# Two weight rests of the output projection: from VectorE to GpSimd, in both layers of the first block

## The reference, cut to what matters

```python
p = jnp.einsum('btd,dc->btc', h, w_in[l])
pa, pb, pc, pd = _split(p, MIXER_COLS)
ya = _hgrn2_mixer(pa, ...); yb = _gla_mixer(pb, ...)
yc, v_first = _rwkv7_mixer(pc, ...); yd = _retnet_mixer(pd, ...)
mix = jnp.einsum('btc,cd->btd', jnp.concatenate([ya, yb, yc, yd], axis=-1), w_out[l])
h = _layer_norm(DN_ALPHA * h + mix, ln1_g[l], ln1_b[l])
```

## Time and profile before

| | |
|---|---|
| median of 3 runs | 3009.65 us |
| the profiled execution | 3002.6 us |
| its core's span | 3000.8 us |
| TensorE busy | 2778.2 us, 93% |
| VectorE busy | 1542.7 us, 51% |
| ScalarE busy | 1085.3 us, 36% |
| GpSimd busy | 208.7 us, 7% |
| mean granted TensorE clock | 0.95 of full |

### The profile page before, as it was taken

One profiled execution on the slowest core, in us unless ns is written; L12 is line 12 of the kernel. 1 busy time (PEld: TensorE's weight loads), 2 busy tenths in 40 slices (PEclk: granted clock), 3 DMA queues, 4 the chain that ended last, 5 costly groups with the idle time before them and its releaser, 6 DMA issues. The chain is left out here.

```text
span 3000.8 us, 38408 instructions
## 1 busy us (share of the span) xinstructions
PE 2778.2 (93%) x14780; PEld 2374.6 (79%) x14780; DVE 1542.7 (51%) x2136; ACT 1085.3 (36%) x1524; POOL 208.7 (7%) x205
## 2 busy tenths in 40 slices
PE   7999999999999999969999999949999896899999
PEld 5779877878877798858988888848878784788787
DVE  3526674232444366647777777763232516732333
ACT  2334223222233242225555555532122416431222
POOL 0011200000000112050000000210000002000000
PEclk9999999999999998879999999979999996899999
DMA  4310025142233000238888888953242210251521
GB/s 151 102 48 1 29 71 140 50 135 79 74 88 97 31 1 29 85 118 237 248 239 235 236 235 237 266 146 91 76 128 74 67 50 20 84 142 48 148 67 67
DMA packets 435565, 335.24 MB, mean 112 GB/s; under 512 B 23488, under 2 KB 375744, under 8 KB 435312
## 3 DMA queue, kind: packets, MB, share of 16 engines
q1 hardware_dynamic: 429360, 318.14, 36.8%
q0 software_dynamic: 3008, 10.09, 1.0%
q10 hardware_dynamic: 3072, 5.24, 0.5%
HBM read 323.43 MB, written 9.99 MB: 111 GB/s over the span
## 5 line engine op out<-in xcount | busy, mean ns | idle before, releaser
L2438 PE MATMUL psum<-x_split,gate_up_split 128*128 128x512 f32 x1056 | 416.5, 394 | 13.9 <-DVE h_tok L2548 5.3
L2439 PE MATMUL psum<-x_split,gate_up_split 128*128 128x512 f32 x1056 | 415.1, 393 | 0.0
L2440 PE MATMUL psum<-x_split,gate_up_split 128*128 128x512 f32 x1056 | 415.0, 393 | 0.0
L3510 PE MATMUL psum<-x_slots_split,gate_up_split 128*128 128x320 f32 x1424 | 378.2, 344 | 16.1 <-DVE gate_up_split L3731 12.4
L3511 PE MATMUL psum<-x_slots_split,gate_up_split 128*128 128x160 f32 x1424 | 314.4, 241 | 0.0
L2561 DVE TENSOR_TENSOR arena<-arena,psum 128x512 f32<-128x512 f32 x66 | 45.3, 687 | 517.0 <-ACT arena L2503 517.0
L3510 PEld LDWEIGHTS psum<-x_slots_split,gate_up_split 128*128 128x128 f32 x1424 | 260.7, 189 | 25.2 <-issue 23.0
L2771 PE MATMUL psum<-x_split,w_split 128*128 128x512 f32 x1152 | 269.7, 393 | 11.6 <-DVE w_split L2808 6.2
L2771 PEld LDWEIGHTS psum<-x_split,w_split 128*128 128x128 f32 x1152 | 215.4, 189 | 66.0 <-issue 15.1
L3511 PEld LDWEIGHTS psum<-x_slots_split,gate_up_split 128*128 128x128 f32 x1424 | 264.2, 191 | 1.8
L2503 ACT ACTIVATE arena<-psum 128x512 f32<-128x512 f32 x66 | 39.5, 598 | 624.5 <-PE psum L2440 624.5
(11 more groups left out here) (518 smaller groups left out, 4725.9 us busy)
## 6 DMA issues: line engine op xcount, KB each, us to landing
arena<-in_moe_w_gate SPq DMA_DIRECT2D x91, 512.0 KB, 4.3
arena<-in_moe_w_up SPq DMA_DIRECT2D x91, 512.0 KB, 5.7
arena<-in_moe_w_down SPq DMA_DIRECT2D x176, 256.0 KB, 5.1
arena<-in_ffn_w_gu SPq DMA_DIRECT2D x88, 512.0 KB, 5.3
arena<-in_w_in SPq DMA_DIRECT2D x32, 1024.0 KB, 5.3
arena<-in_ffn_w_down SPq DMA_DIRECT2D x108, 256.0 KB, 5.2
arena<-in_ffn_w_gate SPq DMA_DIRECT2D x22, 512.0 KB, 4.1
arena<-in_ffn_w_up SPq DMA_DIRECT2D x22, 512.0 KB, 5.5
```

Of the source, the lines that this page charges most:

```text
L2438: nc.tensor.matmul(out, w[0], XR[:, 0, k, :], start=k == 0, stop=False)
L2439: nc.tensor.matmul(out, w[0], XR[:, 1, k, :], start=False, stop=False)
L2440: mm = nc.tensor.matmul(out, w[1], XR[:, 0, k, :], start=False, stop=k == DT - 1)
L3510: hi = lambda start, stop: nc.tensor.matmul(out, wt[0], XE[:, k8, :, :].rearrange("p s n -> p (s n)"), start=start, stop=stop)
```

## The change

Pieces 1 and 0 get their rests on GpSimd, by a new function `pool_piece` that is `dve_piece` with another engine. The two calls stand at the end of GpSimd's list. VectorE's two calls go. Pieces 2 and 3 stay on VectorE (`dve_first_half`). As two engines now add to the count `lo`, ScalarE waits ahead of rounding piece 2 for `lo` to be 2, which also keeps VectorE's rests of pieces 2 and 3 behind GpSimd's.

```diff
--- before.py
+++ after.py
@@ -2090,7 +2090,14 @@
             nc.scalar.wait_ge(*self.R.out_mm.at(TT))
         if p == 0:
             nc.scalar.wait_ge(*self.R.gate_ready.at(1))
+        if p == 2:
+            nc.scalar.wait_ge(*self.lo.at(2))
         nc.scalar.activation(self.k.WMIX[p][:, 0, :], self.raw[p], ACT.Copy).then_inc(*self.hi.up())
+
+    def pool_piece(self, p):
+        nc, W = self.nc, self.k.WMIX[p]
+        nc.gpsimd.wait_ge(*self.hi.at(self.nth(p)))
+        nc.gpsimd.tensor_tensor(W[:, 1, :], self.raw[p], W[:, 0, :].bitcast(F32), ALU.subtract).then_inc(*self.lo.up())
 
     def dve_piece(self, p):
         nc, W = self.nc, self.k.WMIX[p]
@@ -2937,6 +2944,8 @@
                 L.pool_gate()
                 R.pool_extra()
                 L.pool_diagonal()
+                O.pool_piece(1)
+                O.pool_piece(0)
 
             @block.tensor
             def _(pe):
@@ -3160,7 +3169,6 @@
                 L.dve_update(5)
                 H.dve_scale()
                 L.dve_update(6)
-                O.dve_piece(1)
                 R.dve_centre()
                 H.dve_gate()
                 L.dve_state(0)
@@ -3181,7 +3189,6 @@
                 L.dve_scale()
                 L.dve_gate()
                 O.dve_group(0)
-                O.dve_piece(0)
                 O.dve_group(1)
                 O.dve_first_half()
                 O.dve_second_half()
```

## The result

The changed kernel took 3024.65 us (median of 14 runs, 3003.66 to 3028.43), the kernel before beside it 3007.59 us (14 runs, 3000.63 to 3021.22). Their ratio is 1.0042, with a 95% interval of 1.0023 to 1.0061: about 12.6 us slower, 7 to 18 by the interval. The two medians lie further apart, 17.1 us. Three executions that took far longer than all others of their kernel (3538.6 and 4034.64 us of the kernel before, 6968.74 us of the kernel with piece 0 alone) are left out of the ratios. The profiled execution has a span of 3022.4 us.

A forecast was written before the change was run, and what follows sets the result against it. TensorE was taken to set the pace once the output projection's products begin, so their start, behind VectorE's chain, matters. Layer 0 +4.5 and layer 1 +2.35 sum to +6.85 us on 3009.65: 3016.5 us, range 3010 to 3021.

The forecast's parts named there:

- The views: End of the mixer stage, both layers: TensorE alone sets the pace once the output projection's products have begun.
- (b): Piece 0's rest leaves VectorE in a stretch where TensorE is full, in both layers: gain 0.
- (c): GpSimd makes both rests behind GLA's diagonals, 4.5 us each, early enough that TensorE waits for neither piece.
- part (a): Piece 1's rest, 2.28 us, leaves VectorE: 1.05 us gained at L347 in layer 0, nothing in layer 1.
- Part (d): GpSimd's long rests shut out VectorE's L263 and L275: first products +4.5 us in layer 0, +2.35 in layer 1.
- The choice between the bounds: L263 waits and GpSimd precedes L275: +6.85 us; otherwise +4.2 (L263 not stopped) or +5.45 (VectorE first at L273).
- my 0.2 for slower by more: Whole kernel: chance 0.2 of being slower by more than about 0.3%, 9.0 us.
- rival 3: First products: waits lower TensorE's clock, 12 more slow products per layer; +11.5 us, 3021.1 us; chance 0.17.
- The port costs nothing: GpSimd's rests beside VectorE: no waits, only the 1.05 us gain at L347; 3008.6 us; chance 0.07.
- The milder hand-over: L263 not stopped, VectorE first at L273, or a shorter instruction: +3 to +5.5 us, say 3014.2; chance 0.28.
- The clock's 11.5 us: First products: 6.85 us of waits plus 4.6 us for slow products at TensorE's low clock; chance 0.17.
- TensorE waits for a rest made late: Output projection: the change fails its purpose; piece 1 would need to be 12 us late; chance 0.01.

The follow-up runs named there:

- piece 0 alone: Changed kernel with only piece 0's rest on GpSimd, piece 1's back on VectorE; ratio to the kernel before 1.0024 (1.0012 to 1.0037).
- the kernel without any rests: Changed kernel with rests of pieces 1 and 0 made by nobody, GpSimd only counting up; ratio to the kernel before 1.0007 (0.999 to 1.0023).
- write-only kernel: Changed kernel with GpSimd's two subtractions replaced by memsets of about 4.5 us per piece; ratio to the kernel before 0.9995 (0.9979 to 1.0011).
- the kernel in which only VectorE waits: Kernel before, but VectorE makes piece 1's rest twice between L273 and L275, no GpSimd; ratio to before 1.0028 (1.0008 to 1.0047).
- the kernels with short hand-overs: Changed kernel with GpSimd's subtractions as memsets, or each cut into eight of 256 elements; ratios to the kernel before 0.9995 and 0.9993.

## Why the prediction was right, and where it was low

**The views and parts (b) and (c): right; part (a) right in layer 1.** Behind the first product TensorE's row has no wait in either layer (48 products in 11.04 us, as before), and the rests were ready at 395.3 and 402.8 us, 17 and 24 us ahead of their first use. Taking 4.6 us per layer off VectorE gave nothing that can be told, as the kernel without any rests shows (0.999 to 1.0023). The 1.05 us of (a) appears in L347's start where TensorE is at the full clock, and in no measured time.

**Part (d): right in mechanism and place.** L275 was forecast at some 5.7 us and took 5.42 to 5.55 in four profiles; GpSimd's rests at 4.5 us took 4.50 to 4.52 and, where they queued, 5.30 to 5.43. HGRN's gate fell from 1.64 to 1.22 us, as forecast. L263 took 1.75 to 3.45 us, until GpSimd's instruction was over; "over 2 us" failed where TensorE's low clock brought L263 later. The choice between the bounds, that even a tensor_scalar of 128x16 waits, and that GpSimd gets in ahead of L275, held in all four profiles of the changed kernel, in both layers. Only in three of these eight places had GpSimd waited while L273 ran, as forecast; in five its row begins just as L273 ends, some 0.04 us ahead of L275. With piece 0 alone in layer 0 it was L273 that was shut out. The write-only kernel splits the mechanism: the two-input instructions wait for reads, the tensor_scalar also for writes.

**The sum.** Forecast +4.5 and +2.35 us; the profile that was compared has +4.9 and +2.7, the means over all profiles +4.0 and +1.5. The idle time that absorbs part of the wait is set by TensorE's clock in GLA's products, and differs from one execution to the next; I had read it from one.

**The size of the whole: low.** The forecast was a median of 3016.5 us, from 3010 to 3021. The median measured, 3024.65 us, lies above that range, though the kernel before came out 2 us faster than its 3009.65. The ratio says 12.6 us (7 to 18) and, measured again, 8.1 us (1.5 to 14.7), against the 6.85 forecast and the 5.5 to 7.6 of the distances. The forecast lies at the lower edge of the first interval and well inside the second, so how close it came depends on the set. The ratio's first value is above the 9 us that I called the limit of the measurement, its second below; my 0.2 for slower by more was too little by how it came out first. The remainder goes with TensorE's clock: over all runs its mean is 0.9436 and 0.9452 in the two sets of the changed kernel, 0.9474 and 0.9466 in two sets of the kernel before, and 0.9443 in the kernel in which only VectorE waits. That is rival 3's direction, but not its place: the first 12 products took 4.38 to 5.43 us in the profiles of the changed kernel and 4.44 to 5.11 before. Where the clock is lost was not found; the profiles differ by 15 us ahead of the stage alone, more than what is sought.

The three profiles of the kernel before and the four of the changed one do show where the remainder is not. From the first product to the end of the third piece's products both take the same, 36.2 to 36.9 us before and 36.1 to 37.2 changed. From there to layer 1's L484 the kernel before takes 763 to 767 us and the changed one 757 to 767. Behind layer 1's third piece it is 1736.0 to 1739.6 against 1738.7 to 1742.2 us, 2.4 more on average, in ranges that overlap. The largest difference, 4.2 us on average, is ahead of layer 0's L484, where the two kernels are the same.

The first ratio's interval (7 to 18 us) covers the 7.6 us of the compared profiles but not the 5.5 us of the means, the second covers both, so whether there is an extra loss at all stays open. One candidate is untested: in executions without a profile the kernel before may more often have the full clock there, where the kernels with short hand-overs have distances of 19.8 and 21.0 us, and so lose more to the wait than these three profiles show.

**Rivals.** "The port costs nothing" fell with L275's 5.42 us. The milder hand-over occurred in no profile of the changed kernel; its +3 to +5.5 us would fit the second ratio, so it fell by the rows and not by the time. The clock's 11.5 us would fit the first ratio as well as the forecast does or better, but the extra slow dozen of products that it rests on did not appear. "TensorE waits for a rest made late" fell with the rests ready 17 and 24 us early.

## What to carry to other kernels

Before a VectorE instruction is moved to an idle GpSimd, look at what VectorE does in the stretch where GpSimd will run: here a two-input instruction on SBUF that came while GpSimd read SBUF waited for the end of GpSimd's instruction, and a small tensor_scalar did so even where GpSimd only wrote. A long move beside a busy chain can therefore cost the chain up to its whole length, less the idle time further down: here 4.2 us at one instruction for a rest of 4.5 us. If the move is wanted, cut GpSimd's instruction to the size of wait that the chain can take, or start it behind the chain. And an engine's busy share is no gain to be had: here 9.1 us less VectorE work gave nothing that could be told, since 4.6 us of it lay where TensorE was full, and in most of the rest VectorE then waited for TensorE instead.

## What the runs showed of the hardware

- A GpSimd TENSOR_TENSOR of 128x2048 held off a VectorE TENSOR_TENSOR until its end (L275 5.42 us instead of 1.22). Eight of 128x256 in its place held each two-input instruction off by 0.4 to 0.5 us.
- Memsets of GpSimd did not touch two-input VectorE instructions (1.22 us), but did delay a 128x16 TENSOR_SCALAR by 0.6 to 0.7 us.
- An instruction that is held off counts as running in the trace, on either engine: 5.42 us for VectorE's 1.22 us of work, 5.30 us for 4.5 us of GpSimd's, and 8.48 us for eight that yield.
- The same GLA products of TensorE took 0.65 or 1.17 us per pair at its two clock levels, 2.4 and 1.2 GHz, in the same place of different executions (layer 0 of the changed kernel: 1.17 us in its first profile, 0.65 in its second). With it the distance to the first product moved by 3 to 6 us, as much as the effect under study.
